# A two-layer hybrid attention and mixture-of-experts network: the attention stage's short-lived tiles use PSUM banks 0 and 1 in turn

## The reference

```python
qa, ka, va, qd, kd, vd, glu, gates = project_branches(h, w_in, ...)    # one input projection
o_mla  = softmax(qa ka^T * scale_a) va            # 8 heads
o_diff = rms_norm((softmax(q1 k1^T) - lam * softmax(q2 k2^T)) vd)      # 4 heads, two maps each
o_conv = silu(layer_norm(depthwise_conv(a * sigmoid(g))))
g = sigmoid(gates)                                # three gates per channel
y = g[0] * (o_mla @ w_o_mla) + g[1] * (o_conv @ w_o_conv) + g[2] * (o_diff @ w_o_diff)
x = x + g1 * (y @ w_out)
x = x + g2 * mixture_of_experts(rms_norm(x) ...)  # 32 experts, 2 per token
```

## Time and profile before

| | us |
|---|---|
| median of 3 runs | 1594.91 (1593.22 to 1598.25) |
| the profiled execution, device time | 1598.0 |
| its span in the trace | 1596.2 |
| PE busy | 1474.7 (92%) |
| attention stage, layer 0 | about 239 to 505 |
| attention stage, layer 1 | about 1109 to 1267 |

### The profile page before, as it was taken

One profiled execution on the slowest core, in us unless ns is written; L12 is line 12 of the kernel. 1 busy time (PEld: TensorE's weight loads), 2 busy tenths in 40 slices (PEclk: granted clock), 3 DMA queues, 4 the chain that ended last, 5 costly groups with the idle time before them and its releaser, 6 DMA issues.

```text
span 1596.2 us, 19739 instructions
## 1 busy us (share of the span) xinstructions
PE 1474.7 (92%) x7954; PEld 825.1 (52%) x7954; DVE 629.0 (39%) x1461; ACT 384.8 (24%) x827; POOL 142.9 (9%) x104
## 2 busy tenths in 40 slices
PE   5999999999999999989998869999989999898885
PEld 3444335444444445665544446734657785555553
DVE  2469934433234203433111137792443214333223
ACT  4112414422222102212221133222522203011111
POOL 0001410000001110012221110041000110000000
PEclk9999999999999999999998989999999999899998
DMA  9423331112222315289999975635114338799995
GB/s 388 165 106 135 162 129 82 53 53 106 106 106 100 162 39 239 79 324 417 417 420 419 394 280 228 242 148 206 53 53 159 149 126 337 277 420 421 420 419 213
DMA packets 49038, 349.23 MB, mean 219 GB/s; under 512 B 7968, under 2 KB 8480, under 8 KB 17328
## 3 DMA queue, kind: packets, MB, share of 16 engines
q1 hardware_dynamic: 43344, 337.42, 52.3%
q0 software_dynamic: 5024, 8.40, 1.4%
q10 hardware_dynamic: 576, 2.10, 0.3%
HBM read 345.00 MB, written 11.80 MB: 224 GB/s over the span
## 4 chain that ended last, share of the span: by engine, by line
PE 77%; DMA 11%; DVE 4%; ACT 3%; SPq 3%; issue 1%; DVEq 0%; POOLq 0%; ACTq 0%
PE bank L351 74%; DMA arena<-w_up_in 7%; ACT arena L1077 3%; DMA arena<-w_down_in 2%; PE bank L637 2%; SPq L2419 1%; DVE arena L1487 1%; DMA arena<-glu_in 1%; SPq L2428 1%; DMA arena<-ada_in 1%; PE bank L424 1%; PE bank L974 1%; DMA x<-x_in 0%; DVE am L1747 0%; DVE arena L1729 0%
## 5 line engine op out<-in xcount | busy, mean ns | idle before, releaser
L351 PE MATMUL bank<-arena 128*128 128x512 f32 (+10 forms) x6104 | 1275.1, 453 | 61.4 <-DMA arena<-w_up_in 20.0
L351 PEld LDWEIGHTS bank<-arena 128*128 128x128 f32 (+4 forms) x6104 | 668.9, 161 | 579.6 <-issue 411.7
L1077 ACT ACTIVATE arena<-bank 128x512 f32<-128x512 f32 (+5 forms) x454 | 220.9, 504 | 1029.0 <-PE bank L351 916.9
L1487 DVE SCALAR_TENSOR_TENSOR arena<-arena,bank 64x256 f32<-64x256 f32 (+2 forms) x121 | 58.1, 480 | 449.5 <-ACT arena L1077 267.5
L1487 DVE SCALAR_TENSOR_TENSOR arena<-arena,vec 128x512 f32<-128x512 f32 (+1 forms) x254 | 173.4, 757 | 0.4
L1747 DVE TENSOR_REDUCE am<-bank 128x1 f32<-128x512 f32 (+1 forms) x96 | 55.5, 599 | 169.4 <-PE bank L351 169.4
L2275 POOL TENSOR_TENSOR arena<-arena 128x512 f32<-128x512 f32 (+1 forms) x32 | 31.8, 995 | 574.6 <-DVE arena L1487 574.6
L1077 ACT ACTIVATE arena<-bank,am 128x512 f32<-128x512 f32 (+1 forms) x96 | 58.6, 613 | 76.8 <-DVE am L1750 76.7
L2314 POOL DMA_INDIRECT y<-arena,routing x33 | 33.3, 1010 | 188.8 <-ACT arena L1077 183.9
L351 PE MATMUL bank<-arena,silz 128*32 128x512 f32 x384 | 46.1, 598 | 4.3 <-DMA arena<-ada_in 2.7
L637 PEld LDWEIGHTS bank<-con,arena 128*128 128x128 f32 x240 | 29.2, 141 | 37.1 <-issue 24.2
(11 more groups left out here) (177 smaller groups left out, 672.4 us busy)
## 6 DMA issues: line engine op xcount, KB each, us to landing
arena<-w_down_in SPq DMA_DIRECT2D x65, 1024.0 KB, 17.8
arena<-w_gate_in SPq DMA_DIRECT2D x61, 1024.0 KB, 15.9
arena<-w_up_in SPq DMA_DIRECT2D x61, 1024.0 KB, 18.0
arena<-ada_in SPq DMA_DIRECT2D x24, 2048.0 KB, 8.5
arena<-mg_in SPq DMA_DIRECT2D x12, 2048.0 KB, 7.5
arena<-mo_in SPq DMA_DIRECT2D x6, 2048.0 KB, 10.3
arena<-glu_in SPq DMA_DIRECT2D x4, 2048.0 KB, 12.7
arena<-out_w_in SPq DMA_DIRECT2D x4, 2048.0 KB, 15.4
```

The lines of the kernel that those rows point to most:

```text
L351: return nc.tensor.matmul(out, w, rhs, start=start, stop=stop)
L1077: return nc.scalar.activation(out, in_, fn, **kw)
L1487: return V.scalar_tensor_tensor(out, in0, sc, in1, op0=op0, op1=op1)
```

## The change

`NARROW` goes. In the attention stage `begin` ignores the class and gives every new tile the bank that the last one did not use: 0 and 1 in turn, by the parity of all tiles begun so far. `newest` therefore notes for each bank which class its last tile had, and `begin` waits on that class's counter. The order of instructions on every engine stays as it was.

```diff
-        NARROW = {"a": (0,), "d": (1,)}
+        SHARED = (0, 1)
...
-                bank = pools[b][n % len(pools[b])]
+                if shared:
+                    bank = SHARED[(len(number["a"]) + len(number["d"])) % 2]
+                else:
+                    bank = pools[b][n % len(pools[b])]
                 if bank in newest:
-                    pe.wait_ge(empty[b], newest[bank])
-                newest[bank] = n
+                    last_class, last_n = newest[bank]
+                    pe.wait_ge(empty[last_class], last_n)
+                newest[bank] = (b, n)
...
                 all_empty()
-                pools.update(NARROW)
+                shared.append(l)
...
                 values_d(len(DU) - 1)
-                pools.update(WIDE)
+                shared.clear()
```

More of the change, by code:

```diff
@@ L323, in _ @@
             newest = {}
+            shared = []
             def begin(b, name):
```

## The result

The changed kernel takes 1582.16 us (median of 6 runs, 1579.39 to 1585.73), the kernel before 1597.96 us (6 runs, 1593.22 to 1603.82). The ratio is 0.9902, 95% interval 0.9878 to 0.9926: 15.7 us or 1.0% faster (15.8 us between the medians). The ratios given here are not the quotients of the two medians, and can differ from them by some 0.2%; where that matters both are named. The profiled execution of the changed kernel took 1582.35 us with a span of 1580.5.

A forecast was written before the change was run, and what follows sets the result against it. PE was taken to bound both attention stages. Removed bank waits give 11.7 us of idle time plus 5.2 of drain, 16.9 in sum, with added waits and bookkeeping at 0: 1594.9 - 16.9 = 1578.0 us, range 1573 to 1587.

The forecast's parts named there:

- PE bounds both stages: Both attention stages: PE is the bound, busy 258.1 of 266 us in layer 0 and 146.0 of 158 in layer 1.
- All 20 waits: PE's idle times before a tile following one of its class, both attention stages: removing them saves 11.7 us of idle time.
- 13 waits for DVE: PE waiting in attention until DVE has emptied the tile before; in layer 1 these were put at 6.3 us.
- The waits for ACT: PE waiting in attention until ACT has emptied a gate tile; in layer 1 put at 1.4 us, 3 x 0.47.
- The price, idle time plus 0.26 us of drain: Each stalled tile in attention also hides 0.26 us of draining shown as busy: 20 x 0.26 = 5.2 us more gain.
- 4.8 and 12.1 us: Forecast gains of the attention stages in layer 0 and layer 1, idle time and drain together, 16.9 us in sum.
- The new waits: In attention each tile now waits for the one two places before it, possibly of the other class: cost 0.
- The three waits for probabilities: PE's waits for DVE before transposes, 2.02 and 1.81 us in layer 0, 2.74 in layer 1: move with PE, length unchanged.
- The third: Layer 1's long wait of 2.74 us before transposes, at 1184.66 before the change, forecast to come at 1177.5.
- The experts' stages start earlier and swallow nothing: After attention: the experts' weight stream starts when PE frees its buffers, so it starts earlier by as much as PE.
- Slower by the clock: Rival, chance 0.04: PE's clock falls more often in attention; at a mean clock of 0.90 the time would be 1621 us.
- No change: Rival, chance 0.10: the experts' streams swallow attention's gain, leaving 1594.9 us, or 1590.1 if layer 1 alone loses all.

## Why the prediction held

The forecast was 1578 us and 16.9 us of gain; measured were 1582.2 us and 15.7 us of gain. Of the 4.2 us between the two times, 3.1 are the starting point: the kernel before had a median of 1594.91 us over the 3 runs that the forecast used and 1597.96 over 6. The other 1.2 us are gain that did not arrive.

- PE bounds both stages, and the idle time in front of a tile that follows one of its class is a bank wait: right. All 20 waits went, and a later emptying by 0.6 us lengthened 12 of the 13 waits for DVE by just that. The waits for ACT were not tested in this way.
- The price, idle time plus 0.26 us of drain: right. 4.8 and 12.1 us were forecast; 4.8 and 12.1 were measured with the clock taken out, 4.9 and 12.6 in the kernels that change one layer. PE's busy time in the second half of layer 1's stage fell by the drains and the clock's share.
- The new waits cost 0: right, also with 0.6 us more of emptying.
- The three waits for probabilities move with PE and keep their length: right (2.02, 1.81, 2.75). The third was forecast at 1177.5 and came at 1179.85: 0.6 us of later start and 1.7 us of half clock in layer 0.
- The experts' stages start earlier and swallow nothing: right for the whole change, within about a microsecond. In the execution that was profiled with layer 0 alone, 2.9 of its 4.9 us were lost between the stages, but its median was 4.4 us under before.
- Not foreseen: the clock. It was taken as unchanged in both stages. A stretch of 3.4 us moved from one to the other. That the sum did not change was luck: both profiled executions had 6.8 us at half clock in the two stages, but the one with a later emptying in the kernel before had 10.3 and the one with a single bank 20.5.
- Slower by the clock: refuted here. The changed kernel goes round two banks at a mean clock of 0.99 and 1.00, and the kernel with one bank for everything was slower than the one before and longer at half clock. By the rule that the prediction cites from the Trainium skill ("TensorE: Matmul & The Clock Gate", "A second HAM failure mode: psum-queue depth-cycling") going round banks would have been a loss. The traces here do not bear that out: alternating took PE's pauses away.
- No change: refuted by the ratio and its interval. The bank waits here were on PE's path with no DMA wait over them. In the Trainium skill ("TensorE: Matmul & The Clock Gate", "HAM oscillation — how this bites in real kernels") a second PSUM buffer gave no further gain in another kernel; this case does not agree, with 1.0%.
- 1.2 us short of the forecast at the end: 0.6 before attention begins and 0.7 in the experts' stage of layer 1. These were not tested; the kernels do not differ there, and the profiled executions differ by more than that among themselves (608.2 to 613.7 us between the stages, 332.0 to 337.9 behind them). That the whole time came within 1.2 us of the forecast is therefore in part luck; the stage lengths are the firmer support.

## What to carry to other kernels

A bank wait is priced by the idle time in front of the next tile plus the drain that the stalled tile shows as busy: compare a stalled row's time with that of a twice as long one. Two banks for two kinds of tiles serve better in turn than one each, as long as the readers finish one tile within the time of the next (here up to about 1.0 us of emptying under a tile of 1.73). Once the bank waits are gone, look at who the next releaser is: the waits left here, filled, gave another 0.7% by the ratios, and moving independent work into them cost no bank.

## What the runs showed of the hardware

The same wait of PE does not always bring the clock down. Behind 1.81 us of idle time in layer 0 the granted clock stayed at 1.00 before and fell in the changed kernel (0.66 on the mean of 5 us); behind 2.02 us it fell in both (a mean of 0.79 from 282 to 290 in either), but not in the two kernels with the banks alternating in one layer alone; behind 2.74 us it fell before and not in the changed kernel. In all kernels that were run, a fall in the attention stages lasted 3.4 us, or 6.8 (once with the banks alternating in layer 1 alone, twice with one bank for everything). It cost half of its length: layer 0's stage was 3.4 us shorter without its 6.8 us. Where all three long waits were filled, it never fell in the stages. The window of the kernel with alternating banks in layer 0 alone, behind this wait (2.01 us):

```profile
282.00:290.00 8.00, 6.55 (x26) 3.36 (x27) 3.99 (x15) 6.23 (x13) 0.00 (x0) 1.00 0.00 0
```

What decides between the two outcomes stays open; equal waits gave both. With the later emptying in the changed kernel it even fell at the start of layer 1's stage, where the waits ahead of it are 0.81 and 0.68 us (a mean of 0.79 from 1106 to 1114).
